# Products of constants on the tensor engine ahead of its waits, in a one-core kernel of two transformer blocks and their experts

## The reference

```python
def first_block(...):                      # DEPTH = 2 layers
    for l in range(DEPTH):
        h = rms_norm(x, g_mix[l])
        q_a, k_a, v_a, u_b, cq_c, ckv_c, kpe_c, gate_logits = jnp.split(h @ w_in[l], ...)
        y_a = swa_attention(...)           # window attention, 8 heads
        y_b = conformer_conv(...)          # depthwise convolution, 31 taps
        y_c = mla_attention(...)           # latent attention, 8 heads
        x = x + einsum(gates, branches(y_a, y_b, y_c)) @ w_out[l]
        h = rms_norm(x, g_mlp[l])
        x = x + square(relu(h @ w_up[l])) @ w_down[l]
    return rms_norm(x, g_final)

def second_block(...):                     # i = 0: retention and neighbourhood attention; i = 1: pooling
    for i in range(2):
        y = _mixer_retention_na(...) if i == 0 else _pool_mixer(...)
        h = _post_norm(h, m[2] * y, ...)
        h = _post_norm(h, m[5] * _hier_moe(...), ...)   # 32 experts, 2 a token
    return h
```

## Time and profile before

| | us |
|---|---|
| median of three runs | 2226.35 |
| lowest and highest | 2225.97, 2227.18 |
| the profiled execution, its own time | 2227.84 |
| its span, first to last instruction | 2226.1 |
| mean granted clock of TensorE in it (share of 2.4 GHz) | 0.983 |

### The profile page before, as it was taken

One profiled execution on the slowest core, in us unless ns is written; L12 is line 12 of the kernel. 1 busy time (PEld: TensorE's weight loads), 2 busy tenths in 40 slices (PEclk: granted clock), 3 DMA queues, 4 the chain that ended last, 5 costly groups with the idle time before them and its releaser, 6 DMA issues.

```text
span 2226.1 us, 30636 instructions
## 1 busy us (share of the span) xinstructions
PE 2089.9 (94%) x12726; PEld 1446.1 (65%) x12726; DVE 947.8 (43%) x1872; ACT 565.6 (25%) x1056; POOL 0.8 (0%) x6
## 2 busy tenths in 40 slices
PE   7999999999999999999988899999987799999986
PEld 6867779998877789998976444443334444443333
DVE  7899735552743345566365411211113521211112
ACT  2124123331135033344345311111112311111112
POOL 0000000000000000000000000000000000000000
PEclk9999999999999999999999999999999999999999
DMA  6435664446435654433240999999999599999995
GB/s 269 154 152 227 249 243 152 186 175 260 170 117 214 251 205 181 188 122 154 78 188 28 409 420 427 426 425 428 424 426 427 197 422 424 427 425 428 426 426 212
DMA packets 50077, 621.20 MB, mean 279 GB/s; under 512 B 5552, under 2 KB 5680, under 8 KB 12080
## 3 DMA queue, kind: packets, MB, share of 16 engines
q1 hardware_dynamic: 49824, 619.53, 67.9%
q10 hardware_dynamic: 144, 0.13, 0.0%
HBM read 618.59 MB, written 1.05 MB: 278 GB/s over the span
## 4 chain that ended last, share of the span: by engine, by line
PE 73%; DMA 15%; DVE 9%; ACT 2%; issue 1%; SPq 0%; ACTq 0%; DVEq 0%
PE bank L650 19%; DMA ring<-in_experts 12%; PE bank L1315 12%; PE bank L1338 7%; DVE wide L1983 3%; PE bank L863 3%; PE bank L864 3%; PE bank L865 3%; DMA arena<-in_experts 3%; PE sums L865 3%; PE sums L864 3%; PE sums L863 3%; PE sums L1348 2%; PE bank L1006 2%; PE bank L1008 2%; PE bank L1007 2%
## 5 line engine op out<-in xcount | busy, mean ns | idle before, releaser
L650 PE MATMUL bank<-h,ring 128*128 128x256 f32 x1568 | 347.1, 382 | 0.0
L650 PEld LDWEIGHTS bank<-h,ring 128*128 128x128 f32 x1568 | 298.1, 191 | 48.3 <-issue 6.5
L2220 DVE TENSOR_TENSOR ring_split<-ring,arena_split 128x2048 fp32r<-128x2048 f32 x64 | 144.1, 2288 | 149.5 <-ACT arena_split L1604 149.5
L2676 DVE TENSOR_TENSOR wide<-bank,wide 128x256 f32<-128x256 f32 x64 | 27.2, 425 | 386.7 <-ACT wide L1801 386.7
L2683 DVE SCALAR_TENSOR_TENSOR scratch_split<-bank,small,wide_split 128x512 fp32r<-128x512 f32 x64 | 48.0, 750 | 272.4 <-ACT wide_split L1809 272.4
L1604 ACT ACTIVATE arena_split<-ring 128x2048 fp32r<-128x2048 f32 x64 | 119.3, 1906 | 156.6 <-PE sums L865 144.1
L1315 PE MATMUL bank<-ring,h 128*64 128x512 f32 x640 | 143.6, 595 | 15.2 <-DMA ring<-in_experts 15.2
L863 PE MATMUL bank<-h_split,arena_split 128*128 128x256 f32 x512 | 147.6, 288 | 7.1 <-DVE scratch_split L2243 7.1
L864 PE MATMUL bank<-scratch_split,arena_split 128*128 128x256 f32 x512 | 146.7, 287 | 0.0
L865 PE MATMUL bank<-h_split,ring_split 128*128 128x256 f32 x512 | 146.6, 286 | 0.0
L1315 PE MATMUL bank<-arena,wide 128*64 128x512 f32 x608 | 137.0, 595 | 9.8 <-DMA arena<-in_experts 9.7
(11 more groups left out here) (382 smaller groups left out, 3544.1 us busy)
## 6 DMA issues: line engine op xcount, KB each, us to landing
ring<-in_stream SPq DMA_DIRECT2D x99, 2048.0 KB, 7.6
ring<-in_experts SPq DMA_DIRECT2D x96, 2048.0 KB, 29.1
arena<-in_experts SPq DMA_DIRECT2D x72, 2048.0 KB, 26.9
arena<-in_experts SPq DMA_DIRECT2D x22, 1024.0 KB, 23.9
stat<-in_experts SPq DMA_DIRECT2D x22, 512.0 KB, 24.7
scratch<-in_experts SPq DMA_DIRECT2D x22, 512.0 KB, 26.5
extra<-in_experts SPq DMA_DIRECT2D x2, 2048.0 KB, 26.1
arena<-in_stream SPq DMA_DIRECT2D x1, 2048.0 KB, 29.1
```

The costliest lines, as they stand in the source:

```text
L650: mm = pe.matmul(dst, a, b, start=(first and i == 0), stop=(i == len(terms) - 1))
L2220: dve.tensor_tensor(split["ring"][:, slot, 2048 * part:2048 * part + 2048], v, HI[("up", "down")[part]][:, j % 2, :].bitcast(F32), ALU.sub ...
```

## The change

A helper is added that issues n products of the identity with 256 columns of `con` into half of a PSUM bank that nobody reads there. It has no wait and gives no semaphore. It is called at ten places of the program, most of them passed more than once, ahead of a wait of the tensor engine, for 104 products in all. Nothing else is changed. "Ninth slot" in the change's name refers to the ring of the kernel before, which has it already.

```diff
+            def keep_clock(n, dump=sums[2]):
+
+                for _ in range(n):
+                    pe.matmul(dump[:, T:2 * T], ident, con[:, 0:T], start=True, stop=True, skip_group_check=True)
+
...
                 rms_sum(("mix", l))
+                if l == 0:
+                    keep_clock(8)
...
                 for pair in range(HEADS + 2):
+                    if l == 0 and pair == HEADS // 2 - 1:
+                        keep_clock(6)
                     if pair < HEADS:
                         scores(l, pair)
...
                 for c in MOD_CONV:
                     mod_site(l, c)
+                keep_clock(3)
                 S.wait(pe, "y_ready", "conv", l)
...
                 mod_site(l, MOD_MLP[1])
+                keep_clock(7)
                 if l == 0:
                     S.wait(pe, "dve_setup", "zero_ready")
                 mlp(l)
...
                 filled(mm, "sum", "post", i, s)
+                keep_clock(3)
                 bank = open_bank(pe, "sum2", "post", i, s)
...
                 filled(mm, "sum2", "post", i, s)
+                if (i, s) != (1, 1):
+                    keep_clock(10)
...
                 rows(0, 1)
                 rows(1, 1)
+                keep_clock(7)
 
                 S.wait(pe, "members", i)
...
                 filled(product(bank[:, 64:96], [(every, member_r[:, 0, :]), (every, member_r[:, 1, :])]), "rank", i)
+                keep_clock(2, sums[1])
                 zero_sums("read", "rank", i)
...
+                keep_clock(3, banks[3])
                 pe.wait_ge(S.sem(f"moe{i}_y_kept"), rounds * EXPERTS + 1)
                 spread(1, last=True)
...
             pool_rows(3)
+            keep_clock(4)
             pool_band_of(2)
```

## The result

The changed kernel takes 2216.19 us (median of six runs, 2213.38 to 2217.74), the kernel before on the same chips 2226.76. The ratio is 0.9948, with a 95% interval of 0.9936 to 0.996: 10.6 us less by the medians. In the profiled executions, by which the forecast was summed, it is 2227.84 − 2216.24 = 11.6 us, where 14.15 were forecast. The median lies 4.0 us above the 2212.2 of the forecast and 1.2 above its own range of 2208 to 2215, and inside 2208 to 2220. The mean granted clock rose from 0.983 to 0.993, and the span is 2214.5.

A forecast was written before the change was run, and what follows sets the result against it. The chain was taken to run through PE in nearly every stage, slowed by half-clock stretches behind waits. Five items sum to 14.15 us, 2227.84 to 2213.7; less 1.5 for the median, 2212.2, range 2208 to 2220.

The forecast's parts named there:

- It doesn't do what it says: Rival: the clock falls all the same, as constant products don't count or idle is left; 2226 us, chance 0.06.
- the products run at 1.2 GHz and overrun: Rival: products at 0.80 to 0.87 us each overrun their gaps, some 32 us over all calls; 2258 us, chance 0.04.
- item 1: Layer 0's first projection: 5.56 us at half clock, half saved and passed on; 2.8 us, bounds 0 and 2.8.
- Item 2: Layer 0's fourth pair of scores: 3.4 us less work, of which 1.5 passes before another wait is last.
- item 3: Each MLP's start: 1.5 us in layer 0 and 0.9 in layer 1, together 2.4, bounds 0 and 4.2.
- item 5: The pooling: 5.52 us at half clock with PE busy throughout; 2.8 us saved, bounds 1.4 and 2.8.
- item 4: Each moe's head: router 0.85 us plus gathers 1.9, 2.75 on PE; 1.9 taken for moe(0), 2.75 for moe(1).
- The hole in the stream: Weight stream of moe(0) around 1255 to 1259: 225 GB/s against 427 over 4.0 us, so 1.9 us can be closed.
- they give nothing and cost nothing: Products before the convolution's branch, behind `pool_rows(3)` and in each moe's last turn: no half-clock stretch follows, so costed at nothing.
- The rival of moving falls: Long half-clock stretches were that execution's, or uncovered falls last longer; about 10 us remain, 2216.4 us, chance 0.14.
- Part of it is absorbed: Rival: layer 0's vector chain takes back 4.3 us and moe(0)'s weight stream 1.9; 8 us gained, 2218.4 us, chance 0.16.

The follow-up runs named there:

- e4: The changed kernel with two more products behind `zero_sums` in each moe; 2213.41 us, ratio 0.9929 to the kernel before.
- e9: The changed kernel timed again, unedited, beside two other versions on one chip; 2214.95 us, ratio 0.994 to the kernel before.
- e1: The changed kernel without the 34 products that had been costed at nothing; 2218.73 us, ratio 0.9952 to the kernel before.
- e2: The changed kernel with only the first block's three places keeping their products, none in the second block; 2223.09 us, ratio 0.9975 to the kernel before.
- e10: e4's kernel timed again, beside two other versions on one chip; 2212.96 us, ratio 0.9934 to the kernel before.
- e7: e4's kernel with four more products at the very start, ahead of the first sum; 2212.89 us, ratio 0.9937 to the kernel before.
- e8: e7's kernel with more products in the gaps of the second block's attention and ahead of layer 0's last attention transposes; 2216.03 us, ratio 0.9949.
- e11: e7's kernel timed again, beside two other versions on one chip; 2213.3 us, ratio 0.9935 to the kernel before.
- e3: The changed kernel with every count of products halved, rounded down; 2220.6 us, ratio 0.9962 to the kernel before.

## Why the prediction was right, and where not

**Right: the mechanism and the price.** A product of constants costs 0.44 us, hides whole in a gap that is longer than its call, and keeps the clock at 1.00 behind it, at every place but the gathers. "It doesn't do what it says" and "the products run at 1.2 GHz and overrun" are out: twenty in a row took 8.8 us and kept the clock.

**Right, in the profiled execution: items 1, 2, 3, 5 and the router's part of item 4.** The forecast 2.8, 1.5, 1.5 + 0.9, 2.8 and twice 0.85 us are 2.7, 1.45, 1.3 + 0.8, 2.7, and 0.8 and 0.65 in the table. Item 2 shows that only part of a saving passes, and that looking for the wait that ends last next gives its size: the bank that ACT empties late is now waited for by PE (L765, 1.8 us), and DVE's wait is the 2.82 that was forecast.

**Mis-sized: the gathers in item 4,** "at the full clock they would end near 1249.5 … 1.9 us. Together 2.75 us at each moe". The gathers' own part was 0.15 and 0.4 us. I had assumed that seven products ahead of `members` and two ahead of `zero_sums` carry the clock over the head of the moe, and had checked the idle but not what fills the rest: thirteen instructions of 32 and 2 columns. The clock fell again, for half as long as before, but now wholly over the gather's products, where the longer stretch of before lay for 3.0 of its 6.8 us over the ranks, `zero_sums` and the waits among them. With the clock kept up the gathers' part was 1.66 and 1.6 us in e4, and 1.7 in `moe(0)` of e9 without any further product. That is somewhat less than my 1.9, and by another path: I had let DVE's first copy of gathered tokens set the start, but in e4 it was done by about 1241.2, ahead of the first expert at 1241.40, and the chain runs from the gathers straight to the first expert:

```profile
1237.52 3.95 PE bank L650 x32
1241.47 2.72 PE bank L1331 x11
```

The hole in the stream was there and closed, but the bound of 2.75 was nearer for `moe(0)` than the 1.9 that I took from the hole.

**Wrong in detail: "they give nothing and cost nothing".** The four products behind `pool_rows(3)` stand ahead of a wait of 2.34 us that had a fall behind it in two of three profiled executions without them, at about 1.7 us. And of the signs, the one that only the stretches at 229 and in the second block's attention would stand at 0.50 did not come true at the gathers and in the experts of `moe(0)`.

**Not forecast:** 0.8 us at the start, where the first sum of squares took 5.48 us and not 6.39, and 0.4 in the second block's attention. e9, the same kernel, had 0.1 in place of the 0.8 (its first h product at −0.10), so that is the execution's luck, not the change's.

So of 14.15 us, 2.4 were missing at the gathers (1.05 − 0.15 and 1.9 − 0.4), 0.6 went in the course of `moe(0)` (e9, the same kernel, lost nothing there, e1 and e2 lost 0.4 and 0.7, e10 gained 0.6, so the execution decides), and 0.8 in small differences; 1.3 came where no term stood (0.8, 0.4 and 0.1): 11.6. A part of the nearness is luck, since the 0.8 at the start came by the execution. The forecast of the median also took 1.5 us off for a profiled execution slower than the others; after the change the two are level (2216.24 and 2216.19).

The rival of moving falls was nearest to the time, with 2216.4, and the runs show it at work: e2 lost 3 us by it in its profiled execution (about 1 us by its median), and the changed kernel's two profiled executions had different falls at the gathers. The shortfall of the changed kernel lies at one place, the gathers, where my cover left the fall to the execution: e9 kept the clock in `moe(0)` with the same calls. There the forecast and that rival are one, and that the cover was too thin is argued from the 5 of 6 against 2 of 12, not shown by one run. "Part of it is absorbed" did not happen: neither layer 0's vector chain nor the stream took anything back.

The rule on the clock gate (the Trainium skill, TensorE: Matmul & The Clock Gate, Part 1), that the look at activity does not start with the kernel and so the point of a transition varies, is borne out: one kernel's two profiled executions had falls at the gathers of both moes in one, 3.4 us each, and of `moe(1)` alone in the other, for 6.83 us.

**Open.** What a place needs to be safe isn't found: idles of 2.04 and 2.54 us kept the clock and one of 1.73 lost it, and the wait of 1.78 us at L765 lost it in two of nine profiled executions with full counts in layer 0. Both are among the three kernels with four more products at the start (e7, e8, e11); whether these have to do with it stays open. I had no run in which only the kind of instructions ahead of the gathers was changed, so what lets the clock fall at that place isn't shown either.

## What to carry to other kernels

Read the granted clock by stretches, price each stretch at half its busy time, and follow it to the next wait: where another engine's queue ends last, only part of it passes, and where PE is the bound all of it does. A product without a result is free if its call ends before the wait it stands ahead of, so fill gaps nearly whole, and look at what stands between two filled gaps. A place without a fall in one trace may have one in the next: the same wait of 2.34 us at the pooling had none before, and one in two of the experiments. Look for idle behind each call in a new trace, since a call without any may have overrun, as the one of e8 did. Judge single calls by several executions, since a fall at a thin place comes and goes with the execution, here at 1.5 to 1.7 us each where PE sets the pace.

## What the runs showed of the hardware

- The clock went to 1.2 GHz in a stage without any long wait: at 1237.82, behind 13 instructions of 32 and 2 columns, four more of the helper's between them, and waits of 0.67 and 0.85 us.
- Idle alone does not order the cases: in e3, 2.04 us ahead of layer 0's first h product and 2.54 ahead of the pooling kept 2.4 GHz, and 1.73 us ahead of the fourth scores did not. The same 2.34 us in the pooling kept it in the kernel before and lost it in e1 and e2.
- With the clock at 2.4 GHz over the gathers the first expert of `moe(0)` gained 1.66 us on the router (e4, two products more) or 1.7 (e9, none more), and 0.15 with the clock at 1.2. The weight stream moved 427 and 435 GB/s over the ten us from there, and 399 otherwise.
- A fall of 3.41 us among experts that wait for their weights (1633.76) put PE 1.7 us behind, of which 1.5 were back 11 us later.
